# Value products run tile by tile, three slots behind their transposes, in two attention loops of a one-core kernel

## What is computed

```python
s_win = einsum('bqkgd,bjkd->bkgqj', qb, kb) * scale          # masked to |q - k| <= 128
s_ctx = einsum('bqkgd,bjkd->bkgqj', qb, k_ctx) * scale
p = softmax(concat([sink, s_ctx, s_win]))[..., 1:]
out = einsum('bkgqj,bjkd->bqkgd', p, concat([v_ctx, vb]))
```

```python
s = einsum('bqhd,bkhd->bhqk', q_blk, k) * scale + c_blk[..., None] - cum_k
p = softmax(where(k_pos <= q_pos, s, -inf))
out = einsum('bhqk,bkhd->bqhd', p, v)
```

## Time and profile before

| | us |
|---|---|
| median of 3 runs | 2681.74 (2678.52 to 2687.2) |
| the profiled execution | 2681.17 |
| its span | 2679.2 |
| stretch of `attc` (870 to 1160) | 290 |
| stretch of `attf` (1590 to 1760) | 170 |
| PE, PEld, DVE, ACT, POOL busy, share of the span | 88%, 73%, 54%, 31%, 52% |

### The profile page before, as it was taken

How to read it: one execution, slowest core, us unless ns; L and a number is a source line. 1 busy time by engine, 2 the same in 40 slices (tenths; PEclk the granted TensorE clock), 3 DMA queues, 4 the chain that set the end, 5 groups by cost and what they waited for, 6 DMA issues and landing times. The chain is left out here.

```text
span 2679.2 us, 32266 instructions
## 1 busy us (share of the span) xinstructions
PE 2369.7 (88%) x11279; PEld 1945.6 (73%) x11279; DVE 1436.4 (54%) x2166; ACT 824.5 (31%) x1454; POOL 1388.7 (52%) x1348
## 2 busy tenths in 40 slices
PE   6799998989899888888778967888799999999995
PEld 2588886778787777777656756666578887888874
DVE  1823646557681788857869756737542222222235
ACT  3511112124121777733314336723330000000012
POOL 2436546732524777447547856746473743333350
PEclk9799999989999999989899978988899999999997
DMA  7335434513245655242132476652221311111121
GB/s 264 126 127 157 126 95 158 181 47 111 91 159 168 172 154 144 77 181 83 52 126 88 150 188 185 180 190 71 63 87 51 99 59 42 52 49 52 49 66 63
DMA packets 180542, 306.97 MB, mean 115 GB/s; under 512 B 34908, under 2 KB 73496, under 8 KB 179104
## 3 DMA queue, kind: packets, MB, share of 16 engines
q1 hardware_dynamic: 138912, 219.60, 28.0%
q10 hardware_dynamic: 41472, 85.31, 8.6%
HBM read 248.19 MB, written 56.66 MB: 114 GB/s over the span
## 5 line engine op out<-in xcount | busy, mean ns | idle before, releaser
L922 POOL TENSOR_SCALAR WH<-RAW 128x512 fp32r<-128x512 f32 (+1 forms) x470 | 347.0, 738 | 1009.2 <-PE PS L1035 879.4
L1033 PE MATMUL PS<-HXH,WH 128*128 128x512 f32 (+1 forms) x1904 | 762.1, 400 | 86.7 <-DVE XX L2198 22.9
L1034 PE MATMUL PS<-HXL,WH 128*128 128x512 f32 (+1 forms) x1904 | 752.5, 395 | 0.0
L1035 PE MATMUL PS<-HXH,WL 128*128 128x512 f32 (+1 forms) x1904 | 751.7, 395 | 0.0
L925 POOL TENSOR_TENSOR WL<-RAW,WH 128x512 fp32r<-128x512 f32 (+1 forms) x470 | 646.1, 1375 | 39.2
L1033 PEld LDWEIGHTS PS<-HXH,WH 128*128 128x128 f32 (+1 forms) x1904 | 363.9, 191 | 174.8 <-DVE XX L2198 23.6
L1034 PEld LDWEIGHTS PS<-HXL,WH 128*128 128x128 f32 (+1 forms) x1904 | 363.9, 191 | 79.3 <-issue 2.7
L1035 PEld LDWEIGHTS PS<-HXH,WL 128*128 128x128 f32 (+1 forms) x1904 | 362.8, 191 | 79.2
L2253 DVE TENSOR_TENSOR TM<-PS,TM 128x512 f32<-128x512 f32 x44 | 28.4, 686 | 382.2 <-ACT TM L1710 382.2
L1710 ACT ACTIVATE TM<-PS 128x512 f32<-128x512 f32 x44 | 23.9, 595 | 552.4 <-PE PS L1035 552.4
L1033 PE MATMUL PS<-AHH,WH 128*128 128x512 f32 x352 | 142.1, 404 | 25.3 <-DVE AHL L2257 21.6
(11 more groups left out here) (278 smaller groups left out, 4153.4 us busy)
## 6 DMA issues: line engine op xcount, KB each, us to landing
RAW<-in_ada_w SPq DMA_DIRECT2D x160, 256.0 KB, 2.9
RAW<-in_w_ffn_in SPq DMA_DIRECT2D x224, 128.0 KB, 2.1
RAW<-in_w_in_ab SPq DMA_DIRECT2D x88, 256.0 KB, 2.7
RAW<-in_w_in SPq DMA_DIRECT2D x56, 256.0 KB, 2.6
RAW<-in_w_ffn_out SPq DMA_DIRECT2D x52, 256.0 KB, 2.7
XR<-XX ACTq DMA_DIRECT2D x3, 4096.0 KB, 12.1
XX<-XR ACTq DMA_DIRECT2D x3, 4096.0 KB, 13.1
RAW<-in_w_in_c SPq DMA_DIRECT2D x40, 256.0 KB, 2.6
```

The costliest lines, as they stand in the source:

```text
L922: g.tensor_scalar(WH[:, sw, 0:m], RAW[:, r, 0:m], 1.0, 0.0, ALU.mult, ALU.add).then_inc(gpsimd_done, 1)
L1033: mm(out, wh, xh, start=first, stop=False, **kw)
L1034: mm(out, wh, xl, start=False, stop=False, **kw)
L1035: return mm(out, wl, xh, start=False, stop=last, **kw)
```

## The change

In both loops the value products of a tile run three slots after its transposes (PV_LAG), instead of all tiles of a step in one go. The slots of the transposes are set anew, `OTT_AT` of `attf` goes from 9 to 11. PTH, PTL, PT2H and PT2L keep their sizes (5 and 8 places) and become rings: tile tb takes place tb % PT_RING, and ACT waits for the value product of the tile that had the place before. Tiles are numbered in the order of their slots. PE signals after each tile's value product. In `attc`, DVE does only the first low part of a slot ahead of `mx` and the others after `rc`, and the output addition ahead of `mx`; ACT may do three high parts ahead of `exp`. The wait of `mx` for the transposes of the step before last is for the last tile in the new order.

```diff
-        AT = {"c": {5: [5, 5, 6, 6, 7], 4: [5, 6, 7, 7]},
-              "f": {8: [5, 5, 5, 5, 6, 6, 7, 7], 4: [6, 7, 7, 8]}}
-        PV_AT, OTT_AT, OTA_AT = {"c": 9, "f": 9}, {"c": 11, "f": 9}, {"c": 13, "f": 13}
+        AT = {"c": {5: [5, 5, 6, 7, 7], 4: [5, 5, 7, 7]},
+              "f": {8: [5, 5, 6, 6, 7, 7, 8, 8], 4: [6, 7, 8, 8]}}
+        PV_LAG, OTT_AT, OTA_AT = {"c": 3, "f": 3}, {"c": 11, "f": 11}, {"c": 13, "f": 13}
+        PT_RING = {"c": 5, "f": 8}
...
+        TILES = {w: [x for u, xs in sorted(spread(w).items()) for x in xs] for w in "cf"}
+        TB = {w: {x: n for n, x in enumerate(TILES[w])} for w in "cf"}
...
-                        z = step_at(u, PV_AT["c"], 32)
-                        if z is not None:
...
+                        for z, ti in tiles.get(u - PV_LAG["c"], []):
...
+                            if ti == 0 and z >= 2:
                                 pe.wait_ge(vector_done, upto("pvfree", "c", z - 2))
...
+                            pe.wait_ge(vector_done, upto("ptl", "c", tb))
+                            mm(PS[:, 6 + z % 2, :], VS[:, blk, kv, :], PTH[:, tb % PT_RING["c"], :], start=ti == 0, stop=False)
+                            mm(PS[:, 6 + z % 2, :], VS[:, blk, kv, :], PTL[:, tb % PT_RING["c"], :], start=False,
+                               stop=last).then_inc(products_done, 1)
...
-                if z >= 1:
-
-                    act.wait_ge(products_done, upto("pv", "c", z - 1))
...
+                if tb >= PT_RING["c"]:
+
+                    act.wait_ge(products_done, upto("pvt", "c", tb - PT_RING["c"]))
...
-                        for z, ti in tiles.get(u - 1, []):
+                        for z, ti in tiles.get(u - 1, [])[:1]:
                             low(z, ti)
+                        z = step_at(u, OTA_AT["c"], 32)
+                        if z is not None:
+                            pv_dve(z)
...
-                        z = step_at(u, OTA_AT["c"], 32)
-                        if z is not None:
-                            pv_dve(z)
+                        for z, ti in tiles.get(u - 1, [])[1:]:
+                            low(z, ti)
...
-                                dve.wait_ge(products_done, upto("tr", "f", tcount(s - 1, "f") - 1))
+                                dve.wait_ge(products_done, upto("tr", "f", last_tile(s - 2, "f")))
```

More of the change, by code:

```diff
@@ L615, in spread, with tile_count, last_tile @@
             return tiles
+        TILES = {w: [x for u, xs in sorted(spread(w).items()) for x in xs] for w in "cf"}
+        TB = {w: {x: n for n, x in enumerate(TILES[w])} for w in "cf"}
+        def tile_count(z, which):
+            return tcount(z + 1, which) - tcount(z, which)
+        def last_tile(z, which):
+            return max(TB[which][z, x] for x in range(tile_count(z, which)))
         def step_at(u, at, steps):
@@ L1257, in _ @@
                     tiles = spread("c")
-                    for u in range(4 * 31 + PV_AT["c"] + 1):
+                    for u in range(max(tiles) + PV_LAG["c"] + 1):
                         s, h = u // 4, u % 4
@@ L1317, in _ @@
                     tiles = spread("f")
-                    for u in range(4 * 15 + PV_AT["f"] + 1):
+                    for u in range(max(tiles) + PV_LAG["f"] + 1):
                         s, i4 = u // 4, u % 4
@@ L1341, in _ @@
                             did(products_done, ("sc", "f", u))
-                        z = step_at(u, PV_AT["f"], 16)
-                        if z is not None:
[L1345 to L1358, removed]
+                        for z, j in tiles.get(u - PV_LAG["f"], []):
+                            tb, hd, G = TB["f"][z, j], z // 2, z % 2
+                            c0 = max(0, j - 4 * G) * P
+                            last = j == 4 * G + 3
+                            if j == 0:
+                                pe.wait_ge(v_loaded[hd % 2], upto("vl", hd))
+                                if z >= 2:
+                                    pe.wait_ge(vector_done, upto("pvfree", "f", z - 2))
+                            pe.wait_ge(vector_done, upto("ptl", "f", tb))
+                            mm(PS[:, 6 + z % 2, c0:HALF], VS2[hd % 2][:, j, :], PT2H[:, tb % PT_RING["f"], c0:HALF],
+                               start=j == 0, stop=False, skip_group_check=True)
+                            mm(PS[:, 6 + z % 2, c0:HALF], VS2[hd % 2][:, j, :], PT2L[:, tb % PT_RING["f"], c0:HALF],
+                               start=False, stop=last, skip_group_check=True).then_inc(products_done, 1)
+                            did(products_done, ("pvt", "f", tb), *([("pv", "f", z)] if last else []))
@@ L1359, in _ @@
                         for z, j in tiles.get(u, []):
-                            tb = tcount(z, "f") + j
+                            tb = TB["f"][z, j]
                             if tb >= 2:
@@ L1893, in _ @@
                             store_o(act, z // 4)
-                        for z, ti in tiles.get(u, [])[:2]:
+                        for z, ti in tiles.get(u, [])[:3]:
                             weights_high(z, ti)
@@ L1903, in _ @@
                             did(scalar_done, ("exp", "c", u))
-                        for z, ti in tiles.get(u, [])[2:]:
+                        for z, ti in tiles.get(u, [])[3:]:
                             weights_high(z, ti)
@@ L2434, in low @@
                     def low(z, ti):
-                        tb, p_ = tcount(z, "c") + ti, key_blocks(z)[ti]
+                        tb = TB["c"][z, ti]
+                        w_ = tb % PT_RING["c"]
                         dve.wait_ge(scalar_done, upto("pth", "c", tb))
-                        v.tensor_tensor(PTL[:, p_, :], PS[:, 4 + tb % 2, :], PTH[:, p_, :].bitcast(F32),
+                        v.tensor_tensor(PTL[:, w_, :], PS[:, 4 + tb % 2, :], PTH[:, w_, :].bitcast(F32),
                                         ALU.subtract).then_inc(vector_done, 1)
```

40 lines of the change are left out of this document (16 added, 24 removed).

## The result

The changed kernel takes 2655.97 us, the median of 4 runs (2651.06 to 2660.51), against 2681.16 for the one before (4 runs, 2678.52 to 2687.2): 25.2 us less. The two medians have the ratio 0.9906; the ratio on record for the comparison is 0.9895 with a 95% interval of 0.9875 to 0.9915, which is 23 to 34 us. The profiled execution took 2652.78, 28.4 less than that of before. 2646 was forecast, with a range of 2626 to 2670.

A forecast was written before the change was run, and what follows sets the result against it. No engine is full; the windowed loop is bound by how the engines' orders interlock. Windowed 23, loop end 1 and causal 11 make 35 us off 2681.17: 2646, range 2626 to 2670.

The forecast's parts named there:

- The windowed term: Windowed loop: 37.6 us of DVE waits go, less 10.8 for GpSimd and 4 for lumps: 23, plus 1 at the end.
- The wait for `exp`: Windowed loop: output addition ahead of `mx` covers DVE's 0.47 us wait a step; 13.4 us go.
- The wait for high parts: Windowed loop: spreading value products takes 1.84 us off a DVE wait of 0.64; all 24.2 us go.
- GpSimd's 10.8: Windowed loop: GpSimd's 7.76 us of work paces steps with side tiles; 24.5 steps lose 0.44 each, 10.8 us.
- The causal term: Causal loop: 13.3 - 3.2 + 1.5 = 11.6 us gained, taken as 11; ends 3 and 20.
- 3.2 us more: Causal loop: `mx` waits 0.25 to 0.5 us in all 14 steps for the last transposes reading its row buffer.
- if the high parts swallow it: Causal loop: lower end of the gain, 3 us, if waits for high parts take up what is gained.
- The new waits: Both loops: ACT's wait for a ring place and PE's 200 added signals cost nothing; taken as 0.
- SP's queue: Causal loop: side tiles behind the later values' loads still land just in time; 0, or up to 2 us a head.
- The gain lasts: After either loop: what follows starts from the loop's end, not from a transfer under way, so the gain stays.
- The slower rival: Windowed `attc`: low parts behind `mx` hold a PSUM bank, delaying transposes ahead of scores; 2686 us, up to 2700; chance 0.07.
- The signs: Both loops: steps 8.1, then 7.6 to 7.8; high-part wait under 8, `exp` under 5; heads 16 to 17 us.

The follow-up runs named there:

- g4: The kernel before with the windowed attention's new transpose slots and new VectorE order, value products still in one go: windowed loop 259.4 us, whole 2670.13 us.
- e5: The kernel before with only VectorE's new order in the windowed attention, value products in one go: windowed loop 271.5 us, whole 2685.49 us.
- e6: The changed kernel with GpSimd working on 64 instead of 512 columns of most windowed side tiles: windowed loop 245.9 us, whole 2652.22 us.
- e3: The changed kernel with causal transposes at slots 5, 5, 6, 6, 7, 7, 7, 7 and 6, 7, 7, 7: causal loop 162.0 us, 2661.72 us in rounds.
- e8: The changed kernel with the causal attention's old transpose slots, value products still tile by tile: causal loop 158.6 us, whole 2660.58 us.
- h2: The changed kernel with VectorE's windowed order also in the causal attention: causal loop 160.3 us, 2664.94 us in rounds, ratio 0.9903 to before.
- e2: The changed kernel with the windowed parts undone, only the causal attention changed: causal loop 153.2 us, windowed 273.4 us, whole 2682.72 us.
- e4: The changed kernel with DVE's old order in the windowed attention, new slots and tile by tile products kept: windowed loop 260.6 us, whole 2672.60 us.

## Why the prediction was right, point by point

**The windowed term, 23 + 1, measured 24.3**, of which 2.0 are the half clock that the profile of before had and this one had not: the size is right, and of its three parts two are not. *The wait for `exp`* (13.4): right, it went to 0.8 and g4 prices order and slots at 11.2. But its condition was missing. I called the cover of the output addition enough; e5 shows that the order brings nothing in the old slots. *The wait for high parts* (24.2 "in all"): the step that failed. 1.84 off a wait of 0.64 ends it in inner steps, and I stretched that to all steps; the steps of four tiles keep 0.3 to 0.6 us each time, 9.1 in sum, and the products bring 13.1. *GpSimd's 10.8*: wrong. I took its 7.76 of work for a bound on the step, but it was read beside waits and with the 0.17 us pause between a scaling and the side tile behind it, and GpSimd ran its inner steps at 7.6 in the changed kernel (1029.63, 1037.24, 1044.86) with no idle time but those pauses; taking a third of its busy time away moved nothing (e6). DVE is full by itself at 7.5. So 37.6 - 10.8 - 4 came near the measured time by luck: one term was too large and another too large against it.

**The causal term, 11, measured 4.5 in the loop and 2.4 with the rest**: mis-sized, inside its lower end of 3 or just under it. The wait for scores went as forecast (13.3 to 0.5). What failed is "3.2 us more" for the row buffer: it came to 8.2 (9.7 - 1.5), 0.7 each instead of 0.25 to 0.5. And e3 and e8 show that the reasoning by terms was wrong there: neither the burst nor the row buffer's wait was time of its own, the head being paced by how tiles are put into the slots. The bound "if the high parts swallow it" says what happened in e3. The sum also had no term for the granted clock. A head was to take 16.5, and at full clock it took 16.6 to 17.2; but two of the three heads late in the loop fell to half clock for 3.4 us and took 17.9 and 18.1. So part of the missing 6.5 us is the clock, 2.5 to 4.5 by the estimate above. Up to the first of the three values' loads shown, 1638.58 and 1664.62, the loop had gained only 1.1 us; why so little there is open.

**The new waits**: 0, as taken. In both loops ACT's waits before high parts end on transposes (26.5 us, 42.0 us), none on a value product, and PE issued the same work with 200 more signals in 24 us less. **SP's queue**: 0, right. GpSimd waits for a side tile only at the start of the causal loop, 12.8 us against 12.3 before. **The gain lasts**: right; 441 to 442 us between the loops in both.

**The slower rival** did not come about in the changed kernel, but its mechanism is real: e5 and h2 are it, at 0.75 and 0.79 us a wait in front of the scores. It decides where I said, and it is the slots 5, 5, 6, 7, 7 that keep the windowed loop off it. I had judged it by time to spare, and had not seen that the change's own slots were made for it. **The signs**: steps of 7.95 on average, inner ones 7.5 to 7.6 with GpSimd's side tiles and without, instead of 8.1 and then 7.7; the wait for high parts 9.1 instead of under 8; that for `exp` 0.8; GpSimd's wait for reciprocals did go from 78.0 to 55.7, not nearly to nothing; heads 18.1, 16.6 and 17.9 instead of 16 to 17, the two long ones with half clock.

**The sum**: 35 forecast, 28.4 between the profiled executions and 25.2 between medians. Between the profiled executions nearly all the difference is the causal term, 6.5 us; the 3.2 further to the medians are within the scatter of the runs.

## What to carry to other kernels

In a pipeline of engines that each keep their order, a wait is worth its time only if the engine that it frees finds work: in the windowed loop the order of VectorE alone brought 0, with the right slots 11, with the spread products as well 24. So look for what stands in front of the next engine's critical instruction, not for the longest wait. Where tiles pass through two banks, first spread them over the slots; in the causal loop taking away the burst alone left a head at 18.0 us while four tiles stood in one slot. Before an engine is called the next bound, take a good part of its work away and look. And compare TensorE's granted clock stretch by stretch before a few us are put down to an edit.

## What the runs showed of the hardware that I had not expected

VectorE's gating operation (128 x 1024, both inputs in SBUF) took 1.22 to 1.23 us where it met no operation of GpSimd's side tiles (three times in each of the two kernels). In the kernel before, the other five of the eight started while an addition of GpSimd's side tiles was under way; they took 2.04 to 2.21 us and the addition 1.28 to 1.30, as all 42 of them in that loop did (1.28 to 1.31). In the changed kernel five again met one, but the gating had started first: they took 1.31 to 1.51, and the additions 2.13 to 2.14. So in these ten meetings the operation that started second took 0.8 to 1.0 us longer than without a meeting, and the first 0.3 at most. With the order turned, the changed kernel's median is 1.31 against 2.05:

```profile
L2000 DVE TENSOR_TENSOR OT<-OT,GT x8: 1224/1314/1507, 918.2 to 1131.5; 128x1024 f32<-128x1024 f32 x8
```

The eight together took 14.2 us before and 10.8 now: 3.4 us of DVE's work which no step of the prediction had. With the order of VectorE alone they took 1.23 to 1.27, and the loop gained nothing, so it does not simply add up.

The other is the clock. TensorE was granted half its clock for stretches of 3.4 us in heads in which it was busy for 15.9 of 18.1 and 16.0 of 17.9 us, and these were 1.6 and 1.3 us longer than the head between them, which has none (16.6). The same stretches are in the same heads in e2 (18.4 and 18.0 against 16.6) and e6 (18.1 and 17.9 against 16.6); in e4 two heads with one took 18.3 and 17.7, the one without 17.2. None is in the late heads of the five kernels with the old causal order.
